# Recurrence of a two-block transformer kernel: score levels visited in pairs, with three pairs of arrays

## The reference

```python
q = silu(q); logf = log(lb + (1 - lb) * sigmoid(z)); k = (1 - lb) * sigmoid(-z)   # each direction its own z
decay = exp(where(causal, cumsum(logf)[t] - cumsum(logf)[s], -inf))
scores = einsum("btk,btsk,bsk->bts", q, decay, k); o = scores @ v + carried state
o = (out_forward + out_backward); o = o * rsqrt(mean(o * o) + EPS) * gn_g * silu(g); y = o @ w_out
```

## Time and profile before

| | us |
|---|---|
| runs (three) | 1973.47, 1979.56, 1979.60 |
| median | 1979.56 |
| profiled execution, span | 1972.8 |
| stretch of heads 0 to 6 of the recurrence, about | 1292 to 1534 |
| one head there (heads 1, 2, 3, 5) | 34.0 |
| head 4, with the scales of heads 0 to 3 | 37.7 |

### The profile page before, as it was taken

How to read it: one execution, slowest core, us unless ns; L and a number is a source line. 1 busy time by engine, 2 the same in 40 slices (tenths; PEclk the granted TensorE clock), 3 DMA queues, 4 the chain that set the end, 5 groups by cost and what they waited for, 6 DMA issues and landing times.

```text
span 1972.8 us, 26423 instructions
## 1 busy us (share of the span) xinstructions
PE 1928.1 (98%) x10928; PEld 1505.1 (76%) x10928; DVE 1164.0 (59%) x1900; ACT 764.2 (39%) x1088; POOL 0.2 (0%) x4
## 2 busy tenths in 40 slices
PE   8999989999999999999999999999999999999997
PEld 5677777888888776578888887877777678888886
DVE  4347567756564598867565645367677564344344
ACT  5765545413223321544132233344545543232231
POOL 0000000000000000000000000000000000000000
PEclk9999999999999999999999999999999999999999
DMA  6112311455553245324555542222121133232311
GB/s 257 56 51 86 107 44 54 174 210 191 193 197 145 89 112 153 106 75 171 213 187 197 193 149 89 86 68 72 56 66 66 44 107 107 85 107 86 107 64 43
DMA packets 41264, 229.89 MB, mean 117 GB/s; under 512 B 6260, under 2 KB 7316, under 8 KB 15672
## 3 DMA queue, kind: packets, MB, share of 16 engines
q1 hardware_dynamic: 40184, 226.59, 32.6%
q10 hardware_dynamic: 960, 1.60, 0.2%
HBM read 217.38 MB, written 2.11 MB: 111 GB/s over the span
## 4 chain that ended last, share of the span: by engine, by line
PE 89%; DVE 5%; ACT 3%; issue 1%; DMA 0%; SPq 0%; DVEq 0%; ACTq 0%
PE ps L656 24%; PE ps L658 23%; PE ps L657 23%; PE ps L1171 2%; PE ps L1311 1%; PE ps L984 1%; PE ps L1006 1%; PE ps L1276 1%; DVE wl L2020 1%; PE ps L720 1%; PE ps L724 1%; PE ps L1298 1%; DVE cy L2512 1%; PE ps L721 1%; PE ps L990 1%
## 5 line engine op out<-in xcount | busy, mean ns | idle before, releaser
L656 PE MATMUL ps<-hh,wh 128*128 128x512 f32 x1330 | 540.0, 406 | 7.2 <-DVE hl L2451 5.4
L658 PE MATMUL ps<-hh,wl 128*128 128x512 f32 x1330 | 519.3, 390 | 0.0
L657 PE MATMUL ps<-hl,wh 128*128 128x512 f32 x1330 | 518.7, 390 | 0.0
L2020 DVE TENSOR_TENSOR wl<-raw,wh 128x2048 fp32r<-128x2048 f32 (+2 forms) x187 | 340.6, 1825 | 151.4 <-ACT wh L141 151.4
L141 ACT ACTIVATE wh<-raw 128x2048 fp32r<-128x2048 f32 (+1 forms) x168 | 282.8, 1689 | 335.2 <-PE ps L658 253.0
L656 PEld LDWEIGHTS ps<-hh,wh 128*128 128x128 f32 x1330 | 250.1, 188 | 70.9 <-issue 12.4
L658 PEld LDWEIGHTS ps<-hh,wl 128*128 128x128 f32 x1330 | 249.8, 188 | 53.7
L657 PEld LDWEIGHTS ps<-hl,wh 128*128 128x128 f32 x1330 | 250.4, 188 | 49.8 <-issue 3.1
L2107 DVE SCALAR_TENSOR_TENSOR xT<-ps,mod,xT 128x512 f32<-128x512 f32 (+1 forms) x84 | 60.3, 723 | 149.9 <-PE ps L658 149.4
L656 PE MATMUL ps<-ffnHh,wh 128*128 128x512 f32 x256 | 99.6, 389 | 0.0
L657 PE MATMUL ps<-ffnHl,wh 128*128 128x512 f32 x256 | 99.6, 389 | 0.0
(11 more groups left out here) (429 smaller groups left out, 2584.1 us busy)
## 6 DMA issues: line engine op xcount, KB each, us to landing
raw<-in_m SPq DMA_DIRECT2D x64, 1024.0 KB, 4.9
raw<-in_ada SPq DMA_DIRECT2D x48, 1024.0 KB, 4.9
raw<-in_ffn SPq DMA_DIRECT2D x32, 1024.0 KB, 7.0
raw<-in_hin SPq DMA_DIRECT2D x20, 1024.0 KB, 5.0
raw<-in_win SPq DMA_DIRECT2D x10, 1024.0 KB, 7.0
raw<-in_cin SPq DMA_DIRECT2D x8, 1024.0 KB, 5.3
cus<-cu SPq DMA_DIRECT2D x112, 66.0 KB, 2.1
raw<-in_cw SPq DMA_DIRECT2D x4, 1024.0 KB, 5.0
```

The source lines that it names most:

```text
L656: pe.e.matmul(out, wh[:, k, c], xh(k), start=i == 0, stop=False)
L657: pe.e.matmul(out, wh[:, k, c], xl(k), start=False, stop=False)
L658: t = pe.e.matmul(out, wl[:, k, c], xh(k), start=False, stop=i == n - 1)
L2020: t = dve.e.tensor_tensor(P.WL[p % NSPLIT][:, k, :], P.raw[n % NRAW][:, k, :], P.WH[p % NSPLIT][:, k, :].bitcast(F32), ALU.subtract)
```

## The change

`merged` now walks *visits*, lists of one to three steps, in place of single steps: nothing; `nsum` of the head before with diag and level 0; levels 1 and 2; 3 and 4; 5 and 6; x128 and x256; pv; ns. The numbers of turns behind them are `(4, 6, 6, 6, 5, 4, 1, 0)`, so the visits stand ahead of the turns 4, 10, 16, 22, 27 and 31. The step `g` is no longer held: it stands right behind the turn that completes its projection. PE's four matmuls of sums of squares are now the step `nsum`, ahead of the next head's diagonal; `ns` stays behind turn 31 for DVE's multiply. The upper planes go round three places: `H.W[h % 2]`, `H.WB`, `H.WC`. `step_up(l)` and `act_swap(l)` write level l+1 and wait, by `free_for`, for the last reader of that place: level l-2 (for the first two the x128 and x256 of the head before). `H.tmp` and `H.kk` are laid into two arrays that are free in this stage, which makes room for `H.WC`.

```diff
+    def visits(h):
+        a = [("nsum", h - 1)] if h else []
+        return [[], a + [("diag", h), ("lv", h, 0)], [("lv", h, 1), ("lv", h, 2)], [("lv", h, 3), ("lv", h, 4)],
+                [("lv", h, 5), ("lv", h, 6)], [("x128", h), ("x256", h)], [("pv", h)], [("ns", h)]]
+
     def merged(h, more):
         turns, steps, held = project(h, 3) + project(h + 1, 0, 1, 2), [], [("g", h, 2)]
-        for step, n in zip([None] + scores(h) + [("ns", h)], (4, 1, 4, 3, 3, 3, 3, 3, 3, 2, 2, 1, 0)):
-            steps.append(([step] if step else []) + held)
+        for visit, n in zip(visits(h), (4, 6, 6, 6, 5, 4, 1, 0)):
+            steps.append(visit + held)
             held = []
             for _ in range(n):
                 steps.append(turns.pop(0))
                 _, g, w, q = steps[-1][0]
                 if q == 7 and (g, w) != (h + 1, 2):
-                    held = [("g", g, w)]
+                    steps.append([("g", g, w)])
         return interleave((steps, len(steps)), *([(more, 8)] if more else []))
...
-    more = {4: [[("scs", 4)]] + [[("sc", g), ("scy", g)] for g in range(4)],
+    more = {4: [[], [("scs", 4)]] + [[("sc", g), ("scy", g)] for g in range(4)],
...
 def level_arrays(H, h, l):
-    return H.WB if l % 2 else H.W[h % 2]
+    return (H.W[h % 2], H.WB, H.WC)[l % 3]
+
+def free_for(h, l):
+    if l > 2:
+        return [("lv", h, l - 3)]
+    return [(("x128", h - 1), ("x256", h - 1, 1))[l - 1]] if h else []
...
+        H.WC = sb("hWC", [128, 2, S], where=ph)
-        H.tmp = sb("htmp", [128, S], where=ph)
-        H.kk = sb("hkk", [128, S], where=ph)
+        H.tmp = P.sq[1]
+        H.kk = P.sq[0]
...
-        elif kind == "ns":
+        elif kind == "nsum":
...
     Z, H, B = P.Z, P.H, 2 ** l
-    if l:
-        act.wait_ge(Z.up, 8 * h + l)
-        act.wait_ge(*P.banks.full(("lv", h, l - 1)))
-    else:
-        act.wait_ge(Z.w, 2 * h + 2)
-        if h:
-            act.wait_ge(*P.banks.full(("x128", h - 1)))
+    act.wait_ge(*((Z.up, 8 * h + l) if l else (Z.w, 2 * h + 2)))
+    for read in free_for(h, l + 1):
+        act.wait_ge(*P.banks.full(read))
```

More of the change, by code:

```diff
@@ L323, in hgrn_steps @@
     gate = [x for t in project(7, 3) for x in t]
-    out += [("scs", 3)] + gate[:4] + [("g", 7, 2)] + last[0] + gate[4:7] + last[1] + gate[7:] + [("g", 7, 3), ("hout",)]
+    out += [("nsum", 6), ("scs", 3)] + gate[:4] + [("g", 7, 2)] + last[0] + gate[4:7] + last[1] + gate[7:] + [("g", 7, 3), ("hout",)]
     out += a[0] + last[2] + [("sc", 4), ("part", 3)] + a[1]
@@ L2599, in step_up @@
         f = H.T[:, :, off:off + n] if l else H.F[h % 2][:, :, :]
[L2600 to L2606, removed]
+        dve.wait_ge(*((Z.up, 8 * h + l) if l else (Z.w, 2 * h + 2)))
+        for read in free_for(h, l + 1):
+            dve.wait_ge(*banks.full(read))
         dve.settle()
```

## The result

| | before | after |
|---|---|---|
| median of the runs, us | 1977.8 | 2027.5 |
| lowest to highest, us | 1973.5 to 1979.6 | 2023.0 to 2032.1 |
| span of the profiled execution, us | 1972.8 | 2021.1 |

The ratio after to before is 1.0259, with a 95% interval of 1.0238 to 1.028. The change makes the kernel 50 us slower. The forecast was 37 us slower, 2016 us, with a range of 1995 to 2034 us that held the result near its upper end; the inner range of 2003 to 2027 us just missed it.

A forecast was written before the change was run, and what follows sets the result against it. TensorE's queue was taken to bound the stage. Waits of 46.3 us less 9.5 us of joins gave +36.8 us on the median of 1979.6, so 2016 us; inner range 2003 to 2027, full range 1995 to 2034.

The forecast's parts named there:

- The bound: Heads 0 to 6: TensorE, busy 240.89 of 242 us, sets the time; a wait in its queue costs all its length.
- The joins: Small-matmul bursts put side by side on TensorE: 34 joins at 0.28 us save 9.5 us (6.5 to 12.9).
- The wait of level 2: TensorE waits for step_up(1), whose swap stands behind sigmoid and slab on ScalarE: 2.3 us a steady head.
- The wait of level 4: TensorE waits for step_up(3), behind the sigmoid and multiply of turn 15's projection: 2.6 us a steady head.
- x256: TensorE waits at x256 for the last swap, behind two sigmoids and a slab on ScalarE: 0.8 us a steady head.
- Head 4: ScalarE's scales and table load lengthen the chains: waits of 6.1 us at level 2, 3.7 at level 4; 10.4 in all.
- The diagonal: Sums of squares moved to just ahead of the diagonal, its chain unchanged: 0.2 us of wait a steady head.
- rival 4: TensorE's clock falls behind waits, 1.6 us a fall; 22 us if behind all 14 large waits, 2038 us; chance 0.08.
- only the joins count: Rival for the stage: VectorE and ScalarE run ahead, no waits, only the joins' 9.5 us gain: 1970 us; chance 0.10.
- the two chains: Work queued from turn 7 to level 2 and from turn 15 to level 4, with waits of 2.3 and 2.6 us.
- one chain alone is real: Rival: of the chains to levels 2 and 4 only one makes TensorE wait: +19.3 us, 1999 us; chance 0.10.
- the joins save nothing: Rival: semaphore waits between a visit's bursts make each pay its edges: +46.3 us, 2026 us; chance 0.10.

The follow-up runs named there:

- e_best: As e_ahead, but head 7 ordered as in the changed kernel and head 4's sums of squares and scales put back as before the change: 1968.3 us, ratio 0.9957.
- e_slab: The changed kernel with ScalarE's split of a slab moved from turn 9 to turn 10, behind the swaps of levels 1 and 2: 2008.4 us, ratio 1.0165.
- e_held: The changed kernel with the step g held as before the change, behind the next visit: 2011.6 us, ratio 1.0178.
- e_fill: The changed kernel with plain 128x384 matmuls of constants on TensorE in the two long waits of heads 0 to 6: 2008.3 us, ratio 1.0161.
- e_ahead: The changed kernel with each step_up and swap one level earlier in VectorE's and ScalarE's lists, TensorE's list unchanged: 1978.3 us, ratio 1.0002.

## Why the prediction was right, and where it was short

**The bound** was read rightly: TensorE's queue sets the time of the stage, and a wait put into it costs its length.

**The joins** were right in size: 0.28 forecast, 0.27 measured in `e_best` on average, between the ends of 0.19 and 0.38. Part of that agreement is luck: 0.28 was the middle between two ends, with no row for it, and the average holds a short wait at level 2 that lowers it and 0.16 from x256 that raises it. The two visits of levels without a wait saved 0.27 and 0.33. The Trainium skill (TensorEngine Tiling (Array Packing), Tiling Modes, Key Properties) says that a change of tiling mode drains the engine; a saving from joining bursts of one mode fits that. The page gives no price; that the whole 0.38 would be drain was my reading, and it would have given too much.

**The wait of level 2** was forecast at 2.3 us, with the slab ahead of swap 1. The second burst starts 2.62 us behind the first; the burst itself is 0.27 us, so 2.35 (the row's own idle time, 2.17, counts the burst as longer). `e_slab` took the slab off the chain and the head lost 1.06 us of the 1.1 worked out. **The wait of level 4**, forecast at 2.6: 2.91 from burst to burst, so 2.64; `e_held` showed both parts of its chain, the multiply on VectorE and the swap behind the sigmoid on ScalarE. **x256**: 0.8 forecast; it starts 1.72 us behind x128 in head 2 and 0.89 behind it in `e_best`, where it doesn't wait, so 0.83. **Head 4**: its waits were forecast at 6.1 and 3.7 us, and the rows show 6.11 and 3.44 of idle, or 6.3 and 3.6 counted as above. **The diagonal**, 0.2: the list of waits doesn't have it in the steady heads, but it is there. The diagonal starts 0.14 us behind the end of VectorE's sum of both key planes, as waiting bursts do, and 0.51 behind the start of the sums of squares, a burst that took 0.35 to the next turn before. So at least 0.16 us are a wait:

```profile
1377.14 0.42 PE L1338 MATMUL ps<-nrm_sq,con 128*32 128x128 f32 x8
1377.65 0.43 PE L1273 MATMUL ps<-hq,nrm_sq 128*32 128x32 f32 x29
```

```profile
1376.82 0.69 DVE L2678 TENSOR_TENSOR nrm_sq<-hW 128x512 f32<-128x512 f32 x1
```

By periods, the clean head lost 4.26 us of the 4.5 forecast, and `e_fill`, which has all the waits and no fall of the clock, put its profiled span at 2006.1, 33.3 us above that of before; the forecast for waits and joins was 36.8.

**The step that was mis-sized is the clock.** The sum had nothing for it; it stood as rival 4, at 1.6 us a fall, with a chance of 0.08 for the case in which it decides. The price of a fall was right: the heads with one took 1.5 to 1.6 us more. The number was not. I held against it that 1.4 us of idle had left no mark, and this says nothing on waits of 2.3 to 2.6 us, twice in 8 us. At the fourteen large waits ten falls came in one profile and eight in the other, 15 us by the spans, and that is the difference between 35 and 50. The result lies in the range since the range was made wide enough for several falls, not since the sum foresaw them. The Trainium skill (TensorE: Matmul & The Clock Gate, the HAM clock gate) says that idle time between bursts brings the engine from 2.4 to 1.2 GHz; the windows from 1302 to 1308 us, with the clock down to 0.50 behind a wait of 2.17 us, agree.

**The other rivals.** That only the joins count: no, and `e_best` shows what it takes; the two chains must be got out of the way first. That one chain alone is real: no, both were measured apart. That the joins save nothing: no, by `e_best`; its 2026 us come closest to the 2027.5 measured, but by chance, since the falls of the clock stand in for the joins' gain and the rest.

## What to carry to other kernels

Where one list orders the work of several engines, two steps put side by side for TensorE are put side by side for all of them: look at what each other engine must have done by the second one, and at what else its queue holds in front of that. Give the producers a list position of their own, earlier than their consumer's, before joining the consumers; here that turned 50 us of loss into no change (`e_ahead`), and with the order of the heads 4 and 7 set right into 8 us of gain, 0.4% (`e_best`). And price a wait on a saturated TensorE as its length plus a chance of a fall of the clock: here waits of 2.3 to 2.6 us, two in a head, cost close to 40% more than their length (15 us of clock on 38 us of idle).

## What the runs showed of the hardware beyond what I expected

- TensorE waits of 2.3 to 2.6 us (2.17 and 2.45 us as the rows count idle time) were enough for the granted clock to fall to 0.50 behind them (1302 to 1308 us), 1.5 to 1.6 us of time each, in six of the seven heads, though not behind each wait. Three dummy matmuls of 128x384 in each wait (eight and five in head 4) took all these falls away, and the kernel ran 19 us faster for about 2.2 us of idle work in each wait (a row of 2.20 us).
- Shortening one of the two waits by 0.7 to 1.1 us left four stretches of low clock in the stage (`e_held`) and three (`e_slab`), where the two profiles of the changed kernel have ten and eight. The falls went faster than the waits: `e_held` lost 5 us of queue and 16 us of time.
